# Expert blocks of a routed mixture: two 32-row groups on four column tiles in place of one 64-row block

## The reference, cut to what matters

```
g_idx = argmax(t @ w_rg + b_rg)                     # one group of 4
top_v, top_i = top_k(le_sel, 2)                     # 2 of its 4 experts
hid = silu(t @ w_gate[e]) * (t @ w_up[e])           # 1024 -> 512
out += combine * (hid @ w_down[e])                  # 512 -> 1024
```

## Time and profile before

| | us |
|---|---|
| time, median of 3 runs | 664.36 (660.15 to 665.67) |
| span of the profiled execution, first to last instruction | 658.4 |
| start of the first gate-up product | 308.9 |
| start of the last down product | 577.0 |
| PE busy | 609.9 (93% of the span) |
| mean granted clock of TensorE | 0.973 of full speed |

### The profile page before, as it was taken

How to read it: one execution, slowest core, us unless ns; L and a number is a source line. 1 busy time by engine, 2 the same in 40 slices (tenths; PEclk the granted TensorE clock), 3 DMA queues, 4 the chain that set the end, 5 groups by cost and what they waited for, 6 DMA issues and landing times.

```text
span 658.4 us, 9372 instructions
## 1 busy us (share of the span) xinstructions
PE 609.9 (93%) x3378; PEld 386.6 (59%) x3379; DVE 215.6 (33%) x480; ACT 201.9 (31%) x440; POOL 59.8 (9%) x105
## 2 busy tenths in 40 slices
PE   6999999999999999996899999999999999925995
PEld 6998777879989899953333333333333333304883
DVE  3521265446253442373010111111011110173663
ACT  5532355545444533342100101010010100162774
POOL 0000000000000000002012121221212122110000
PEclk8999999999999999998999999999999999976998
DMA  9833113121111079865999999997998999935001
GB/s 311 223 141 128 67 62 128 64 65 65 65 65 65 1 270 393 310 217 188 368 345 398 397 396 398 342 389 285 397 398 307 389 396 398 408 117 232 32 33 64
DMA packets 76416, 153.34 MB, mean 233 GB/s; under 512 B 7960, under 2 KB 27296, under 8 KB 76128
## 3 DMA queue, kind: packets, MB, share of 16 engines
q1 hardware_dynamic: 72144, 139.77, 58.1%
q0 software_dynamic: 3952, 12.85, 5.1%
q10 hardware_dynamic: 288, 0.28, 0.2%
HBM read 142.66 MB, written 10.23 MB: 232 GB/s over the span
## 4 chain that ended last, share of the span: by engine, by line
PE 80%; DMA 9%; DVE 4%; ACT 2%; SPq 2%; issue 2%; POOLq 0%; DVEq 0%; POOL 0%; ACTq 0%
PE bank L1557 20%; PE bank L1297 13%; PE bank L1298 12%; PE bank L1299 12%; PE bank L1581 10%; DMA ple_gate_raw<-in_w_ple_gate 4%; PE bank L1379 2%; DMA ring_gu<-in_w_up 2%; PE bank L1504 2%; PE bank L1545 2%; SPq L577 2%; PE bank L1352 2%; DMA gmix<-in_norm_mix 1%; PE bank L1393 1%; PE bank L1569 1%
## 5 line engine op out<-in xcount | busy, mean ns | idle before, releaser
L1557 PE MATMUL bank<-ring_gu,rowsT 128*64 128x512 f32 x736 | 164.6, 599 | 3.2 <-issue 1.8
L1557 PEld LDWEIGHTS bank<-ring_gu,rowsT 128*64 128x64 f32 x736 | 50.9, 138 | 100.6 <-issue 99.2
L1581 PE MATMUL bank<-ring_dn,hidT 128*64 128x512 f32 x368 | 84.0, 598 | 1.4 <-DVE hidT L1200 1.4
L865 ACT ACTIVATE silu_g<-bank 128x256 f32<-128x256 f32 x23 | 8.8, 383 | 236.3 <-PE bank L1557 236.3
L1045 DVE TENSOR_TENSOR w_lo<-w_raw,w_hi 128x2048 fp32r<-128x2048 f32 x18 | 41.3, 2292 | 76.9 <-ACT w_hi L730 69.2
L1195 DVE TENSOR_TENSOR hid<-silu_g,bank 128x256 f32<-128x256 f32 x23 | 9.7, 421 | 165.3 <-ACT silu_g L865 165.3
L1297 PE MATMUL bank<-w_hi,hT_hi 128*128 128x256 f32 x192 | 55.7, 290 | 0.8 <-issue 0.8
L1298 PE MATMUL bank<-w_lo,hT_hi 128*128 128x256 f32 x192 | 54.6, 284 | 0.0
L1299 PE MATMUL bank<-w_hi,hT_lo 128*128 128x256 f32 x192 | 54.5, 284 | 0.0
L1297 PE MATMUL bank<-hT_hi,w_hi 128*128 128x512 f32 x128 | 50.8, 397 | 0.0
L1581 PEld LDWEIGHTS bank<-ring_dn,hidT 128*64 128x64 f32 x368 | 24.4, 136 | 44.7 <-issue 44.7
(11 more groups left out here) (210 smaller groups left out, 901.1 us busy)
## 6 DMA issues: line engine op xcount, KB each, us to landing
ring_gu<-in_w_gate SPq DMA_DIRECT2D x32, 1024.0 KB, 13.1
ring_gu<-in_w_up SPq DMA_DIRECT2D x32, 1024.0 KB, 15.2
ring_dn<-in_w_down SPq DMA_DIRECT2D x16, 2048.0 KB, 10.8
w_raw<-in_w_in SPq DMA_DIRECT2D x14, 1024.0 KB, 5.1
w_raw<-in_w_out SPq DMA_DIRECT2D x4, 1024.0 KB, 4.9
ple_gate_raw<-in_w_ple_gate SPq DMA_DIRECT2D x1, 4096.0 KB, 26.1
yg<-y_rows SPq DMA_DIRECT2D x8, 512.0 KB, 7.3
xr<-in_x SPq DMA_DIRECT2D x4, 512.0 KB, 9.3
```

Source lines behind the costliest of these rows:

```text
L1557: last = T.matmul(b_gu[q * BLK:(q + 1) * BLK, :], rowsT[:, k % 4, k // 4, :], ring_gu[s][:, k, :, q * UC:(q + 1) * UC], start=(k == 0), st ...
L1581: last = T.matmul(b_dn[q * BLK:(q + 1) * BLK, :], hidT[:, kf % 2, kf // 2, :], ring_dn[s][:, kf, q * (D // 2):(q + 1) * (D // 2)], start=( ...
```

## The change

A step now takes two groups of GRP = 32 rows. Groups are numbered through all experts; an expert takes ceil(pairs/32) groups, and step b takes the groups 2b and 2b+1, which are of one expert or of two neighbours. The two halves q of the columns and the two groups g make four column tiles of 32, so that each product is written as four with 32 stationary columns instead of two with 64; the moving weights are as wide as before (512) and are streamed once for each tile. The table in SBUF holds the number of loads of each group (`grp_loads`) and a code for the pair of slots (`blk_pair`): three for one expert, three for neighbours, so that PE has six copies of the products instead of three, and loads three values ahead of them instead of two. PE's loop has one step in a turn instead of three. The row buffers become one (`rows`), and POOL gathers block b+1 in place of b+3. Rows that fill up a group are read from two new rows of `h2_rows`.

```
-        rows = [at(f"rows{i}", kb, [P, D // 2]) for i, kb in enumerate((64, 66, 99.25))]
-        rowsT = at("rowsT", 68, [P, 4, 2, BLK])
+        rows = at("rows", 99.25, [P, D // 2])
+        rowsT = at("rowsT", 68, [P, 4, 2, 2, GRP])
...
-            for b in range(ROW_BUFS):
-                gather(b, b, b + 1)
+            gather(0, 0, 1)
             pool.wait_ge(xT_done, 1)
-            gather(ROW_BUFS, 0, ROW_BUFS + 1)
+            gather(1, 1, 2)
             def step(b, k, turn):
                 pool.wait_ge(xT_done, b + 1)
-                gather(b + ROW_BUFS, (1 + k) % ROW_BUFS, 2 * b + ROW_BUFS)
-                scatter(b - 1, k % 2, 2 * b + (ROW_BUFS + 1))
+                gather(b + 1, (2 + k) % 3, 2 * b + 1)
+                scatter(b - 1, k % 2, 2 * b + 2)
...
-            def in_slot(b, products):
-                loads = pe.value_load(blk_loads[0:1, bass.ds(b, 1)], min_val=1, max_val=6)
-                slot = pe.value_load(blk_slot[0:1, bass.ds(b, 1)], min_val=0, max_val=RING - 1)
-                with pe.If(slot < 1):
-                    products(0, loads)
+            def in_slots(b, products):
+                loads = [pe.value_load(grp_loads[0:1, bass.ds(2 * b + g, 1)], min_val=1, max_val=6) for g in range(2)]
+                pair = pe.value_load(blk_pair[0:1, bass.ds(b, 1)], min_val=0, max_val=2 * RING - 1)
+                with pe.If(pair < RING):
+                    with pe.If(pair < 1):
+                        products((0, 0), loads)
...
+                with pe.Else():
+                    with pe.If(pair < RING + 1):
+                        products((0, 1), loads)
...
-            def rows_transpose(b, buf, loads):
-                pe.wait_ge(s_rows[buf], 16 * loads)
+            def rows_transpose(b):
+                pe.wait_ge(s_rows, 16 * (b + 1))
...
-                        for q in range(2):
-                            last = T.matmul(b_gu[q * BLK:(q + 1) * BLK, :], rowsT[:, k % 4, k // 4, :],
-                                            ring_gu[s][:, k, :, q * UC:(q + 1) * UC],
-                                            start=(k == 0), stop=(k == KD - 1))
+                        for g in range(2):
+                            for q in range(2):
+                                o = g * BLK + q * GRP
+                                last = T.matmul(b_gu[o:o + GRP, :], rowsT[:, k % 4, g, k // 4, :],
+                                                ring_gu[slots[g]][:, k, :, q * UC:(q + 1) * UC],
+                                                start=(k == 0), stop=(k == KD - 1))
...
-            over_blocks(pe, total, step, group=PE_GROUP)
+            over_blocks(pe, total, step, group=1)
```

More of the change, by code:

```diff
@@ L420, in trunk @@
         s_plegate = sem("ple_gate_loaded")
-        s_rows = [sem(f"block_rows_loaded{i}") for i in range(ROW_BUFS)]
+        s_rows = sem("block_rows_loaded")
         s_ystored = sem("block_out_stored")
@@ L603, in _ @@
             sp.wait_ge(ple_ready, 2 * NT)
-            for buf in range(ROW_BUFS):
-                sp.wait_ge(s_rows[buf], 16)
+            sp.wait_ge(s_rows, 16)
             load_dn(2, 2)
@@ L664, in gather @@
                 pool.sem_inc(gathers_begun, 1)
-                pool.indirect_dma_start(out=rows[buf][:], out_offset=None, in_=h2_rows,
-                                        in_offset=rows_of).then_inc(s_rows[buf], 16)
+                pool.indirect_dma_start(out=rows[:], out_offset=None, in_=h2_rows,
+                                        in_offset=rows_of).then_inc(s_rows, 16)
             def scatter(b, buf, n_columns):
@@ L1274, in stage6_b @@
                                            ALU.mult).then_inc(res_ready, 1)
-            for buf in range(ROW_BUFS):
-                dve.wait_ge(s_rows[buf], 16 * ((total + (2 * ROW_BUFS - 1 - buf)) // ROW_BUFS))
+            dve.wait_ge(s_rows, 16 * (total + 1))
             stage6_a(0)
@@ L1526, in _, with products @@
             pe.wait_ge(table_ready, 1)
[L1527 to L1534 removed]
+            total = pe.value_load(cum_i[0:1, N_EXPERTS - 1:N_EXPERTS], min_val=N_EXPERTS // 2, max_val=MAX_BLOCKS)
+            def in_slots(b, products):
[5 more added lines that the diff above has]
+                    with pe.Else():
+                        with pe.If(pair < 2):
+                            products((1, 1), loads)
+                        with pe.Else():
+                            products((2, 2), loads)
                 with pe.Else():
[L1536 to L1537 removed]
+                    with pe.If(pair < RING + 1):
+                        products((0, 1), loads)
                     with pe.Else():
[L1539 to L1543 removed]
+                        with pe.If(pair < RING + 2):
+                            products((1, 2), loads)
+                        with pe.Else():
+                            products((2, 0), loads)
+            def rows_transpose(b):
+                pe.wait_ge(s_rows, 16 * (b + 1))
                 for j in range(4):
[L1545 removed]
+                    last = T.transpose(b_xT[:, j * P:(j + 1) * P], rows[:, j * P:(j + 1) * P], ident)
                 last.then_inc(xT_done, 1)
             def gate_up(b):
[L1550 removed]
+                def products(slots, loads):
                     pe.wait_ge(xT_ready, b + 1)
@@ L1562, in products @@
                     last.then_inc(gu_done, 1)
-                in_slot(b, products)
+                in_slots(b, products)
             def hidden_transpose(b):
@@ L1572, in down, with products @@
             def down(b):
-                def products(s, loads):
+                def products(slots, loads):
                     pe.wait_ge(hidT_ready, b + 1)
                     pe.wait_ge(y_ready, b + 1)
-                    pe.wait_ge(s_dn[s], 16 * loads)
+                    pe.wait_ge(s_dn[slots[0]], 16 * loads[0])
+                    if slots[1] != slots[0]:
+                        pe.wait_ge(s_dn[slots[1]], 16 * loads[1])
                     for kf in range(D_EXPERT // P):
-                        for q in range(2):
-                            last = T.matmul(b_dn[q * BLK:(q + 1) * BLK, :], hidT[:, kf % 2, kf // 2, :],
-                                            ring_dn[s][:, kf, q * (D // 2):(q + 1) * (D // 2)],
-                                            start=(kf == 0), stop=(kf == D_EXPERT // P - 1))
+                        for g in range(2):
+                            for q in range(2):
+                                o = g * BLK + q * GRP
+                                last = T.matmul(b_dn[o:o + GRP, :], hidT[:, kf % 2, g, kf // 2, :],
+                                                ring_dn[slots[g]][:, kf, q * (D // 2):(q + 1) * (D // 2)],
+                                                start=(kf == 0), stop=(kf == D_EXPERT // P - 1))
                     last.then_inc(dn_done, 1)
-                in_slot(b, products)
-            rows_transpose(0, 0, 1)
+                in_slots(b, products)
+            rows_transpose(0)
             pe.wait_ge(ple_ready, 2 * NT)
             gate_up(0)
-            rows_transpose(1, 1, 1)
+            rows_transpose(1)
             def step(b, k, turn):
```

128 lines of the change are left out of this document (71 added, 57 removed).

## The result

| | us |
|---|---|
| before, median of 4 runs | 662.25 (660.04 to 665.67) |
| after, median of 4 runs | 777.84 (775.90 to 780.01) |
| ratio, after to before | 1.171 (95% interval 1.168 to 1.174) |
| forecast | 720.0, range 674 to 770 |

The change makes the kernel 17% slower. The direction was forecast, the size was not: the time lies 8 us above the range. The profiled execution took 775.9 us, with a span of 774.1 us. The kernel before took 660.0 and 660.2 us in two of its runs and 664.4 and 665.7 in the others; its profile, with a span of 658.4, is of one of the quicker two, and in it the first gather goes out at 303.9 us, against 306.8 us in the changed kernel and also in e1_old_one_buffer and e11_old_gather_first, which keep the tables of before.

The account below looks back on a forecast made before the run. PE was taken to bound the kernel, with DMA close behind. First down's end 333.0 + 18 x 16.6 + last down 8.4 + evacuation 0.2 + rest 73.6 = 714.0, plus 6.0 around the span: 720 us, range 674 to 770.

Parts of the forecast that it names:

- period P: Time from the end of one down to the end of the next in the expert loop: 16.6 us, 18 times.
- The 6.0 us around the span: Time outside the profiled span, added to the 714.0 us of span to give 720 us.
- Steps: PE's expert loop: 20 steps for 23, taking 34.7 us off PE at an unchanged 11.56 us a step.
- Products: PE's products: four tiles of 32 share the array as two did; gate-up stays 7.02 us, down 3.58.
- The gather: POOL's gather behind the scatter: issued 4.13 us after down, landing 6.2 later, about 2.9 late for PE each step.
- The value loads: PE's sequencer: three loads make sections of 2.9 us before gate-up and 2.8 before down, with 2.2 of cover.
- add 0.4 for the clock: Expert loop: 0.4 us added to each period for PE's clock halving after idleness.
- 0.9 for the longer section and 0.3 for tables make 333.0: Start of the experts: these additions move the end of the first down from 331.8 to 333.0 us.
- The end: After the loop: last down starts 4.8 us after the one before, ends 8.4 after it; 73.6 from evacuation on unchanged.
- That of the clock: Rival for the loop: clock halves in most steps, down up to 1.8 us longer, 745 to 772 us; chance 11%.
- The "faster" rival: Expert loop: gathers and sequencer keep up, PE holds 11.56 us a step, DMA bounds, 644 us; chance 4%.
- The two rivals on tiles and on code in the loop: PE's loop: tiles not shared, about 820 us, chance 8%; code not staying on the core, beyond 770, chance 2%.

Follow-up runs that it names:

- e1_old_one_buffer: The kernel before (64-row blocks), with one row buffer and POOL's order of the changed kernel, gathering b+1 instead of b+3: 771.57 us, ratio 1.163.
- e11_old_gather_first: The kernel before, with one row buffer and the gather of b+2 ahead of the scatter: 663.82 us, ratio 0.999.
- e8_one_value: e2_gather_first plus the edit of e4_two_copies, with one packed value load ahead of each product instead of three: 663.11 us, ratio 0.997.
- e9_new_half_weights: e8_one_value, with weight refills from the fourth expert on moving half of the columns (output not the layer's): 634.47 us, ratio 0.956.
- e2_gather_first: The changed kernel, still with one row buffer, but POOL gathers block b+2 ahead of the scatter: 677.61 us, ratio 1.021.
- e4_two_copies: The changed kernel, with one value load and two product copies instead of six in the first gate-up ahead of the loop: 766.84 us, ratio 1.152.

## Why the prediction was right in kind and short in size

The span was forecast at 714.0 and came out at 774.1. Its terms:

| term | forecast | measured | on the span |
|---|---|---|---|
| end of the first down | 333.0 | 352.1 | +19.1 |
| period P, 18 times | 16.6 | 18.88 | +41.0 |
| last down after the one before | 8.4 | 7.7 | -0.7 |
| evacuation and rest | 73.8 | 74.5 | +0.7 |

714.0 + 60.1 = 774.1. The 6.0 us around the span was too much: this execution took 1.8 more than its span. The other 4.2 stood for the difference between the median of before and its profiled execution, whose first gather goes out 2.9 us earlier than here; most of them belong to the first row.

**Steps.** Right: 20 steps, and e8_one_value and e9_new_half_weights show that they cost 11.53 us each where neither rows nor weights are late.

**Products.** Right: gate-up takes 7.07 us and down 3.64 at the whole clock. The Trainium skill's figure for array packing ("TensorEngine Tiling (Array Packing)", Theoretical Speedup), up to 4 times for 32 columns, is borne out from two tiles to four: 64 matmuls of gate-up end in 7.07 us, where 32 of the same width took 7.09. No run here has one tile alone beside them. The prediction's sum of single times, 32 x 599 ns against 7.02 us, proves less than it says: 64 x 608 ns is 5.5 times 7.07 us with four tiles, so the records of single matmuls overlap inside a tile too.

**The gather.** Right in place and mechanism: 4.18 us to its issue (forecast 4.13), and e1, e2 and e11 show that this order makes and unmakes the loss. Its landing was a little short. The parts of P have means of 4.18 to the issue, 6.00 to land, 0.04, 3.12 from the transposes to down, and 5.53 of down, in sum 18.87; for the landing 6.2 less 0.6 for quiet queues was taken, so 0.4 too little. Quiet queues were rarer, and full ones dearer, than taken. A weight load often starts just when the gather does, as at 450.65 beside 450.60, since it waits for the first half of gate-up.

**The value loads.** Right: 3.12 us from the transposes' start to down, where 2.8 was taken. With rows in time the cover was short by 0.5 to 1.1 us ahead of gate-up (forecast about 1.5), and by 0 to 0.2 ahead of down (forecast 0.5).

**The clock.** The step "add 0.4 for the clock" failed as a term that was mis-sized. The prediction saw the pattern in the step (idle, short transposes, idle), and had the price in its own rival, up to 1.8 us of down, but gave that 11%. It measured 5.53 - 3.58 = 1.95 on average, so 18 times 1.5 more than taken, or 27 us. This is the larger part of the 2.3 us by which P was off; 0.4 is the landing and 0.3 the sequencer's section. The earlier trace rows showed a case of each kind, and the term was set near the unhalved one, where the new step, with short transposes between two idle stretches, resembled the halved one.

**The first pass.** The step "0.9 for the longer section and 0.3 for tables make 333.0" failed by leaving a term out. The prediction considered code only for the loop's steady state, where its answer (it stays) was right: none came in 352:600. In e11_old_gather_first, which has the first gather at 306.8 us as the changed kernel has, the first down ends at 335.3, so the change itself costs 16.8 us up to there, where 1.2 was taken; the other 3.5 of the 19.1 come with the later first gather, which the change does not make. The 16.8 stand as follows beside that kernel: the second gate-up starts 6.7 later, is 2.6 longer (9.73 us, part of it at half clock), the gap behind it is 6.0 longer, and down is 1.4 longer. In the two gaps lie the three long branches (12.3 us, in part under PE's work) and the longer sections; how much each has was not settled. e4_two_copies took 6.4 away. In e8_one_value D0 is still 5.6 us behind that of e11, with branches of 5.1 and 4.6 us.

**The end.** The small miss here is luck. The last down was to wait 4.8 us for empty turns of the loop and then to take 3.6; in the trace it waits for DVE's copy of its input, starts 2.4 us after the down before it, and takes 5.34 us, at half clock again.

**The rivals.** That of the clock (P of 18 to 19.5, 745 to 772 us) described the loop rightly, with P at 18.88, and missed the time by the first pass: its own formula, 421.2 + 18 P, gives 761. The "faster" rival at 644 asked for the right thing, the gather within reach, which e2_gather_first gave by order and not by a short landing; but with all rows in time DMA held the kernel at 663, not 644. Its terms, 96 MB at 397 GB/s from 314 us on, end at 556 and not near 559; and the stream does not run at 397 from there on. Part of the window 310:350 of e8_one_value, whose four stretches have 297, 351, 132 and 267 GB/s:

```profile
330.00:340.00 10.00, 7.14 (x56) 2.68 (x52) 0.42 (x1) 0.98 (x2) 1.15 (x2) 0.83 0.36 132
```

The two rivals on tiles and on code in the loop are out by the rows above.

## What to carry to other kernels

When buffers are taken away, look not only at how many are left but at what the engine that refills them does first: here the gather stood behind a scatter in program order and waited for what the scatter waits for, and moving it ahead was worth 100 us, with one buffer and with no other edit. When a forecast puts a wait into each step, price the product behind the wait at both clocks: here, with two idle stretches and 0.66 us of transposes between them, down took up to 6.6 us instead of 3.64. And before work is taken off the busiest engine, look at the next one: here DMA stood at 395 to 398 GB/s, and three steps of PE were worth nothing until half the bytes of the refills were gone.

## What the runs showed of the hardware that was not expected

A branch that leads past copies of the products that have not run yet held TensorE's sequencer for 3.2 to 5.8 us in the changed kernel, against 0.07 to 0.22 us for the same branches in 352:600. That the fetch of code is the cause is argued from the eight blocks on q8 in 316:352 and from e4_two_copies, not shown alone.

Dead matmuls made a kernel faster: 3.55 us of them in a step, in place of waiting, gave back 1.9 us of the down that follows and 27 us in all.

A gather of 64 rows landed in 7.2 us with 365 GB/s on the queues, and in 3.3 us with 107 GB/s.
